# A new step table for a decoder trunk: heads at 0.7 of a step, and a router that takes four more steps

## The chip, the cores and the metric

The kernel runs on one core of a Trainium2 chip. Its time is the device time of one execution in microseconds (us), taken as the median of several runs. The core has five engines that run programs of their own and meet at semaphores: TensorE (PE), VectorE (DVE), ScalarE (ACT), GpSimd (POOL) and SyncE (SP), and 16 DMA engines that all queues share.

## The reference

The input x is 512 rows of 1024 columns, in float32. There are two layers. A layer takes x through a modulated RMS norm, a token mixer (six heads of dilated sliding-window attention, a diagonal state-space model on 256 channels, six heads of latent attention), an output projection and a gated residual, and then through an expert retrieval:

```python
def peer_ffn(h, wq, subkeys, u_tab, v_tab):
    q = (hf @ wq).reshape(T, PEER_HEADS, 2, PEER_DKEY // 2)
    scores = jnp.einsum('thjd,hjkd->thjk', q, subkeys)
    top_s, top_i = lax.top_k(scores, PEER_TOPK)                      # 8 heads, 2 sides, 16 of 128
    cand = top_s[:, :, 0, :, None] + top_s[:, :, 1, None, :]
    best_s, best_c = lax.top_k(cand.reshape(...), PEER_TOPK)         # 16 of the sums
    experts = i1 * PEER_KEYS + i2                                    # 128 experts for each row
    gates = softmax(best_s)
    act = gelu(einsum('td,tkd->tk', xt, u_tab[experts]))
    out = einsum('tk,tkd->td', gates * act, v_tab[experts])
```

Each row of x so reads 128 experts of 2048 numbers (a row of u and one of v, laid side by side in memory), in each of the two layers.

## The kernel before, in words

The 512 rows are 4 tiles of 128; with two layers there are 8 tiles of work, numbered 0 to 7 (`TILES`). A tile needs 128 gathers: gather n brings the n-th expert of each of its 128 rows, 128 x 2048 numbers, into one of the 8 places of a ring (`ringbuf`, `RING = 8`). POOL does nothing else (`pool_program`, L638): before gather n it waits until PE has finished with gather n - 8 (`summed`), and before the first gather of a lot until VectorE has written its indices (`idx_done`).

Two gathers are a pair, and a pair is a *step*: 64 steps a tile, 512 in all. For each pair VectorE takes the dot product of both u rows with the normed input (L1846) and a product with the gates (L1849), ScalarE makes of them the weight and two scaled diagonals (L1335 to L1350), and PE adds the two v rows into PSUM with these diagonals, 16 matmuls (L1003), which frees the two places of the ring. At the start of a tile's pairs the sums of the tile before are copied out (`sides`, L1853 and L1355), folded by PE (L1016) and finished by VectorE (L1861, L1862).

The rest of a tile's work (its norm, projections, state-space model, attention, output projection, query projection and scores, then the router, which picks the experts) lies between the pairs of the tile before: this is the *background*. Each of PE, ScalarE and VectorE has one generator `background()` that walks through `tile(j)` for all tiles in a fixed program order, and says by `yield at(j, step)` when its next piece is due. `at(j, step)` is `START[j] + step` in pair numbers. The engine's main loop issues a pair, and the `Feed` issues all background pieces whose due step has come, so a due step between two whole numbers counts as the next whole one; I call what stands between two pairs a slot. On PE the slot's background stands ahead of the slot's pair, on VectorE and ScalarE behind it. No piece overtakes another on its engine, also when the table gives it an earlier step. Everything due before step 0 is done before the first pair, one piece behind the other: the prologue.

`clocks()` gives for each tile its start and its *phase* (the step of its first own pair): phase j is 64 j, and with `LEAD = READY = 58` a tile starts 58 steps before its phase. In table steps of a tile: norm and transposes 0 to 3, projection by eight chunks of `w_in` 3 to 11 on PE and evacuated by ScalarE at 6 to 12, the state-space model on VectorE from 7 to 14, attention preparation to 18, then 12 attention heads in 14 iterations from 19 on, one per step: PE writes the logits of head i, transposes the weights of head i - 1 and mixes head i - 2 (L854, L862, L873), VectorE adds the bias and takes the maximum (L1669), ScalarE takes the exp (L1243) and evacuates the transposed weights (L1234). The bias comes by DMA, one block `BM` for each of the six window heads and one for the six latent ones, in two places, and SP loads block b when head b - 2 has been scored (`lmax`, L588). Behind the heads come the norm of the mix, the output projection, the second norm, and the query projection with its scores, one of eight chunks of `p_wq` each 1.5 steps. SP's queue is a fixed program too, driven by semaphores and not by the table: it loads a chunk as soon as PE has freed its place (`w_done`).

The router runs on VectorE (`route`). For each of 8 heads it takes the 16 best of 128 keys on both sides (two pieces) and the 16 best of the candidate sums (third piece, L1813 and `top16`); then for each lot of two heads (in tile 0 lots of 1, 1, 2, 2, 2) it works out indices and gates in three pieces (`batch`). `route_clock(j)` gives each piece its due step from a running sum of costs in table units: 1.7, 1.7 and 3.3 for a head, 1.0, 2.2 and 3.4 for a lot, 80.0 units for a tile and 86.6 for tile 0. Before, a piece is due at `44.5 + now / 3.14`, so all go at 3.14 units a step; a piece due more than a step behind the phase is put one step later. The router begins 13.5 steps ahead of the phase and is done 11.9 steps behind it (14.0 in tile 0). ScalarE's exp of a lot's gates (`gates`, L1098) is due with the lot's first piece; that of the last lot is merged into ScalarE's program of the next tile, behind head step 3. That next tile starts 6 steps behind the phase.

In tile 3's attention (`j == T - 1`, in the phase of tile 2) the tables of the second layer's state-space model are built: six pieces of `setup(1)` on VectorE from head 5 on, and three on ScalarE at heads 4, 6 and 10, the last with four passes over 128 x 1024 (L1078 to L1081).

## Time and profile before

| | |
|---|---|
| median of 3 runs | 3276.8 us (3274.89 to 3279.24) |
| the profiled execution, in all | 3276.72 us |
| its span, first to last instruction | 3274.9 us |
| busy in the span | PE 71%, VectorE 72%, ScalarE 44%, POOL 35% |
| moved by DMA | 1318.48 MB, 403 GB/s in the mean |
| mean granted clock of TensorE | 0.842 |

### The profile page before, as it was taken

Reading aid. Unit: us, or ns where it says so; the run is one execution under the profiler, and the core shown is the slowest. Engines: PE = TensorE matmul, PEld = TensorE weight load, DVE = VectorE, ACT = ScalarE, POOL = GpSimd, SP = SyncE. Lnnn points to the kernel's source line nnn. Section 1 sums busy time; section 2 is a strip of 40 time slices with the busy share of each in tenths; the row PEclk is TensorE's granted clock in tenths of the full one; section 3 lists DMA queues with packets and bytes.
Section 4 is the critical chain, followed back from the end, with each engine's and each line's share of the span. In section 5 each row is a group of like instructions: output and inputs, shape, how many; then the busy total and the mean of one; then the engine's idle time right before and its main releaser. Section 6 shows DMA issues by size and latency. Waiting matters only on the chain.

```text
span 3274.9 us, 44590 instructions
## 1 busy us (share of the span) xinstructions
PE 2328.0 (71%) x15012; PEld 1150.4 (35%) x15012; DVE 2369.8 (72%) x6467; ACT 1439.0 (44%) x4646; POOL 1143.5 (35%) x1029
## 2 busy tenths in 40 slices
PE   7675777677875777857676677768777577775555
PEld 5362334333442433514243233424335143431111
DVE  6669856797668876688667985688766986688554
ACT  2214454344533456344543445334553446434443
POOL 0003333333433333333443334333443333434443
PEclk9887889879987888869788788888889799877777
DMA  9859999999999999999999999999999999999998
GB/s 374 362 209 374 412 420 420 418 389 420 421 418 409 407 420 380 419 409 418 420 417 417 396 420 421 419 401 405 415 420 419 402 417 421 419 415 393 415 422 332
DMA packets 207467, 1318.48 MB, mean 403 GB/s; under 512 B 26413, under 2 KB 43613, under 8 KB 54150
## 3 DMA queue, kind: packets, MB, share of 16 engines
q0 software_dynamic: 147456, 1073.81, 79.7%
q1 hardware_dynamic: 58918, 241.04, 18.4%
q8 instruction: 119, 1.95, 0.2%
q10 hardware_dynamic: 864, 0.79, 0.1%
q14 instruction: 110, 0.90, 0.1%
HBM read 1310.54 MB, written 7.29 MB: 402 GB/s over the span
## 4 chain that ended last, share of the span: by engine, by line
DMA 38%; DVE 23%; PE 21%; ACT 6%; issue 4%; POOL 3%; ACTq 0%; SPq 0%; POOLq 0%; DVEq 0%
DMA ringbuf<-in_p_uv,IDX 34%; PE PS L1003 11%; DVE ringbuf L1846 11%; POOL ringbuf L638 3%; DMA WB<-in_p_wi 3%; PE PS L935 3%; PE PS L965 2%; PE PS L777 2%; ACT v_th L1338 2%; ACT DIAG L1350 1%; ACT v_w L1343 1%; DVE I L1739 1%; PE PS L736 1%; DVE T L1737 1%; DVE EQ L1783 1%
## 5 line engine op out<-in xcount | busy, mean ns | idle before, releaser
L638 POOL DMA_INDIRECT ringbuf<-in_p_uv,IDX x1024 | 1143.1, 1116 | 2105.9 <-PE PS L1003 1698.0
L1003 PE MATMUL PS<-ringbuf,DIAG 64*64 64x512 f32 x8192 | 1303.3, 764 | 776.0 <-ACT DIAG L1350 752.6
L1846 DVE SCALAR_TENSOR_TENSOR ringbuf<-ringbuf,H 128x1024 f32<-128x1024 f32 x1024 | 1237.5, 1222 | 618.2 <-DMA ringbuf<-in_p_uv,IDX 614.7
L1003 PEld LDWEIGHTS PS<-ringbuf,DIAG 64*64 64x64 f32 x8192 | 313.4, 158 | 1483.0 <-ACT DIAG L1350 1019.5
L1335 ACT ACTIVATE v_sq<-v_y 128x2 f32<-128x2 f32 x512 | 104.1, 203 | 1430.3 <-DVE ringbuf L1846 1430.2
L1343 ACT ACTIVATE v_w<-v_th,v_g 128x1 f32<-128x1 f32 x1024 | 340.5, 379 | 48.6 <-ACT v_th L1338 1.1
L1338 ACT ACTIVATE v_th<-v_sq,v_y 128x1 f32<-128x1 f32 x1024 | 340.5, 380 | 17.2
L1350 ACT ACTIVATE DIAG<-fold,v_w 128x64 f32<-128x64 f32 x1024 | 300.4, 340 | 16.6
L965 PEld LDWEIGHTS PS<-HT,WB 128*128 128x128 f32 x1856 | 227.4, 203 | 66.4 <-issue 61.4
L965 PE MATMUL PS<-HT,WB 128*128 128x128 f32 x1856 | 238.1, 290 | 0.1
L777 PE MATMUL PS<-WB,HT 128*128 128x256 f32 (+2 forms) x816 | 176.1, 371 | 48.7 <-DMA WB<-in_p_wi 43.8
L777 PEld LDWEIGHTS PS<-WB,HT 128*128 128x128 f32 x816 | 146.2, 197 | 102.8 <-DMA WB<-in_p_wi 67.3
L1669 DVE CUSTOM_DVE_ANT_0 PB<-PS,BM 128x128 f32<-128x128 f32 (+3 forms) x96 | 47.1, 491 | 84.0 <-PE PS L854 48.6
L1849 DVE TENSOR_TENSOR v_g<-v_y,GATE 128x2 f32<-128x2 f32 x512 | 82.5, 161 | 17.8
L1846 DVE DVE_READ_ACCUMULATOR ringbuf<-ringbuf,H 128x1 f32 x1024 | 84.0, 82 | 0.0
L1737 DVE MAX8 T<-SC 128x8 f32<-128x128 f32 x256 | 74.0, 289 | 4.4
L1243 ACT ACTIVATE PB<-PB,NMX 128x128 f32<-128x128 f32 (+3 forms) x96 | 53.0, 552 | 50.6 <-DVE NMX L1669 50.3
L1739 DVE FIND_INDEX8 I<-T,SC 128x8 uint32<-128x128 f32 x256 | 72.9, 285 | 0.0
L935 PE MATMUL PS<-KEEP,HT 128*128 128x256 f32 x256 | 60.7, 392 | 3.7 <-ACT HT L1273 3.7
L935 PE MATMUL PS<-WB,HT 128*128 128x256 f32 x256 | 59.2, 385 | 0.0
L935 PEld LDWEIGHTS PS<-KEEP,HT 128*128 128x128 f32 x256 | 48.6, 194 | 23.3 <-issue 17.0
L1234 ACT ACTIVATE PT<-PS 128x128 f32<-128x128 f32 (+3 forms) x96 | 40.3, 420 | 31.2 <-PE PS L862 31.0
(287 smaller groups left out, 2277.3 us busy)
## 6 DMA issues: line engine op xcount, KB each, us to landing
WB<-in_p_wq SPq DMA_DIRECT2D x58, 1024.0 KB, 12.3
WB<-in_p_wi SPq DMA_DIRECT2D x37, 1024.0 KB, 9.6
ringbuf<-in_p_ahead SPq DMA_DIRECT2D x24, 1024.0 KB, 12.2
WB<-in_p_wo SPq DMA_DIRECT2D x16, 1024.0 KB, 9.7
ringbuf<-in_p_uv,IDX POOLq DMA_INDIRECT x1024, 12.6
WB<-in_p_ada SPq DMA_DIRECT2D x12, 1024.0 KB, 12.7
WF<-in_p_ada SPq DMA_DIRECT2D x12, 1024.0 KB, 13.6
WB<-in_p_wi SPq DMA_DIRECT2D x14, 768.0 KB, 8.8
```

The costliest lines, as they stand in the source:

```text
L638: pool.indirect_dma_start(out=ring[n % RING], out_offset=None, in_=table, in_offset=bass.IndirectOffsetOnAxis(ap=IDX[:, k % 2, s:s + 1], a ...
L777: last = pe.matmul(PS[:, 4 + i % 2, 0:w], HT[:, k, :], weights(n)[:, k * w:(k + 1) * w], start=(k == 0), stop=(k == KD - 1))
L935: last = pe.matmul(PS[:, 6 + i % 2, 0:WIDE], HT[:, k, :], wt[:, k * WIDE:(k + 1) * WIDE], start=(k == 0), stop=(k == KD - 1))
L965: last = pe.matmul(PS[:, 4 + i % 2, h * P:(h + 1) * P], weights(n)[:, k * WIDE + h * P:k * WIDE + (h + 1) * P], HT[:, k, :], start=(k == 0 ...
L1003: mm = pe.matmul(PS[half:half + HALF, 2 * c + r, :], DIAG[r * HALF:(r + 1) * HALF, (n + q) % DIAGS, :], row[r * HALF:(r + 1) * HALF, D + c ...
L1335: act.activation(SQY[:, b, :], Y[:, b, :], ACT.Square, scale=GELU_S / GELU_T).then_inc(squared, 1)
L1338: th = link.mark(act.activation(TH[:, b, q:q + 1], SQY[:, b, q:q + 1], ACT.Tanh, scale=Y[:, b, q:q + 1], bias=Y[:, b, q:q + 1]))
L1343: w = link.mark(act.activation(W[:, b, q:q + 1], TH[:, b, q:q + 1], ACT.Identity, scale=G[:, b, q:q + 1], bias=G[:, b, q:q + 1]))
L1350: act.activation(DIAG[:, n % DIAGS, :], fold[:, :], ACT.Copy, scale=W[:, b, q:q + 1])\
L1737: step(dve.max(tops[:, part], values))
L1739: step(dve.max_index(places[:, part], tops[:, part], values))
L1846: dve.scalar_tensor_tensor(row, row, GELU_T, H2[:, k % 2, :], ALU.mult, ALU.mult, accum_out=Y[:, b, q:q + 1]).then_inc(dotted, 1)
```

## The change

Only the step table is changed; no instruction, load or semaphore is added or taken away.

- A tile starts 54 steps before its phase instead of 58 (`LEAD`, `READY`), so 10 steps behind the phase of the tile before.
- The iterations of the heads are due at `19 + 0.7 i` instead of `19 + i`. Counted from the phase they begin at -35 (before: -39) and end at -25.9 (before: -26).
- Everything behind the heads is due 4 table steps earlier, which is the same pair as before (on ScalarE and VectorE the norm of the mix, 32 and 33 before, is due at 28.2 and 29). What lies ahead of the heads keeps its table step, and so comes 4 pairs later.
- The router begins at the same pair, 13.5 steps before the phase. Its first 42 units go at 3.5 units a step, the rest at 2.15. It ends 15.6 steps behind the phase (18.7 in tile 0), before 11.9 (14.0).

```diff
--- before.py
+++ after.py
@@ -170,10 +170,11 @@
     return start, phase
 
 
-LEAD = 58
-READY = 58
+LEAD = 54
+READY = 54
 PERIOD = 64
-ROUTE_RATE = 3.14
+HEAD_STEP = 0.7
+ROUTE_FROM, ROUTE_FAST, ROUTE_SLOW, ROUTE_EARLY = 40.5, 3.5, 2.15, 42.0
 START, PHASE = clocks()
 
 
@@ -188,7 +189,8 @@
 
     def piece(cost):
         nonlocal now
-        at_, now = at(j, 44.5 + now / ROUTE_RATE), now + cost
+        steps = min(now, ROUTE_EARLY) / ROUTE_FAST + max(now - ROUTE_EARLY, 0.0) / ROUTE_SLOW
+        at_, now = at(j, ROUTE_FROM + steps), now + cost
         return at_ + 1 if at_ > PHASE[j] + 1 else at_
 
     for h in range(PH):
                     last.then_inc(omm, 1)
 
                 for i in range(2 * HEADS + 2):
-                    yield at(j, 19 + i)
+                    yield at(j, 19 + HEAD_STEP * i)
                     if i == 0:
                         pe.wait_ge(mla_ev, 3 * (j + 1))
                     if j == 0 and i in (5, 9):
@@ -903,7 +905,7 @@
                         mix(i - 2)
                     if i in (3, 4):
                         side_rows(i - 3)
-                yield at(j, 34)
+                yield at(j, 30)
                 if j == 0:
                     reduce_ahead(3)
                 for c in more[-2:]:
@@ -917,7 +919,7 @@
                     if k % 4 == 3:
                         last.then_inc(mx_tp, 1)
                 for i in range(4):
-                    yield at(j, 35 + i)
+                    yield at(j, 31 + i)
                     if i < KEPT:
                         pe.wait_ge(keep_in, 16 * KEPT * (l + 1))
                         wt, used = KEEP[:, i, :], keep_done
@@ -935,7 +937,7 @@
                         last = pe.matmul(PS[:, 6 + i % 2, 0:WIDE], HT[:, k, :], wt[:, k * WIDE:(k + 1) * WIDE],
                                          start=(k == 0), stop=(k == KD - 1))
                     last.then_inc(used, 1)
-                yield at(j, 41)
+                yield at(j, 37)
                 if j == 0:
                     reduce_ahead(4)
                 pe.wait_ge(n2_h, j + 1)
@@ -956,7 +958,7 @@
                     last.then_inc(s_mm, 1)
 
                 for i in range(PH):
-                    yield at(j, 42 + 1.5 * i)
+                    yield at(j, 38 + 1.5 * i)
                     m, n = PH * j + i, number[("wq", j, i)]
                     pe.wait_ge(w_in[slot[n]], turn[n])
                     pe.wait_ge(q_ev, m - 1) if i >= 2 else pe.wait_ge(n2_ev, 2 * (j + 1))
@@ -970,7 +972,7 @@
                         score(i - 1)
                     if j == 0 and i == 5:
                         reduce_ahead(5)
-                yield at(j, 42 + 1.5 * PH)
+                yield at(j, 38 + 1.5 * PH)
                 score(PH - 1)
 
             def background():
@@ -1235,7 +1237,7 @@
 
                 tables = setup(1) if j == T - 1 else None
                 for i in range(2 * HEADS + 2):
-                    yield at(j, 19 + i)
+                    yield at(j, 19 + HEAD_STEP * i)
                     if tables and i in (4, 6, 10):
                         next(tables, None)
                     if i < 2 * HEADS:
@@ -1254,15 +1256,15 @@
                         ada_keep(more[i - 2], 4 + (i - 1) % 2)
                     if 1 <= i <= len(more):
                         ada_take(more[i - 1])
-                yield at(j, 32)
+                yield at(j, 28.2)
                 for c, lo, hi in ((0, 0, SWA), (1, SWA, SWA + S5C), (2, SWA + S5C, D)):
                     act.wait_ge(at_fin, 2 * j + (1, 1, 2)[c])
                     act.activation(SQ[:, lo:hi], HM[:, lo:hi], ACT.Square, accum_out=V0[:, c:c + 1]).then_inc(mx_ss, 1)
-                yield at(j, 33)
+                yield at(j, 29)
                 act.wait_ge(mx_rs, j + 1)
                 for c, lo, hi in ((0, 0, SWA), (1, SWA, SWA + S5C), (2, SWA + S5C, D)):
                     act.activation(HM[:, lo:hi], HM[:, lo:hi], ACT.Copy, scale=RS[:, c:c + 1]).then_inc(mx_n, 1)
-                yield at(j, 34)
+                yield at(j, 30)
                 if j == 0:
                     keep_ahead(3)
                 if tables:
@@ -1272,10 +1274,10 @@
                         act.wait_ge(mx_tp, 2 * j + k // 4 + 1)
                     act.activation(HT[:, k, :], PS[:, 4 + k // 4, k % 4 * P:(k % 4 + 1) * P], ACT.Copy,
                                    scale=LP[:, LP_MIX + k:LP_MIX + k + 1]).then_inc(mx_ev, 1)
-                yield at(j, 39)
+                yield at(j, 35)
                 act.wait_ge(wo_res, 4 * (j + 1))
                 act.activation(SQ[:, :], XM[:, j % 2, :], ACT.Square, accum_out=VN[:, 1:2]).then_inc(n2_ss, 1)
-                yield at(j, 41)
+                yield at(j, 37)
                 if j == 0:
                     keep_ahead(4)
                 for b in range(2):
@@ -1290,7 +1292,7 @@
 
                 due = [(lot[0], g) for g, lot in enumerate(route_clock(j)[1][:-1])]
                 for i in range(PH + 1):
-                    step = at(j, min(42.5 + 1.5 * i, 42 + 1.5 * PH))
+                    step = at(j, min(38.5 + 1.5 * i, 38 + 1.5 * PH))
                     while due and due[0][0] <= step:
                         b, g = due.pop(0)
                         yield b
@@ -1647,7 +1649,7 @@
 
                 tables = setup(1) if j == T - 1 else None
                 for i in range(2 * HEADS):
-                    yield at(j, 19 + i)
+                    yield at(j, 19 + HEAD_STEP * i)
                     if i == 0:
                         dve.wait_ge(s5_th, j + 1)
                         dve.scalar_tensor_tensor(G5[:, :, :], SQ5[:, :, :], 1.0, YT[:, :, :], ALU.add, ALU.mult)\
@@ -1673,9 +1675,9 @@
                     add_ahead(j, KD // 2)
                     if 2 <= i <= len(more) + 1 and more[i - 2][2] // 4 == 4:
                         row_gain(more[i - 2], 4 + (i - 1) % 2)
-                yield at(j, 32)
+                yield at(j, 28.2)
                 finish(1)
-                yield at(j, 33)
+                yield at(j, 29)
                 dve.wait_ge(mx_ss, 3 * (j + 1))
                 link(dve.tensor_tensor(V0[:, 0:3], V0[:, 0:3], CPK[:, CP_MEANS + 33:CP_MEANS + 36], ALU.mult))
                 link(dve.tensor_scalar(V0[:, 0:3], V0[:, 0:3], EPS, None, ALU.add))
@@ -1684,7 +1686,7 @@
                 if j == 1:
                     column_scale(1)
                 for i in range(4):
-                    yield at(j, 36 + i)
+                    yield at(j, 32 + i)
                     cols = slice(i * WIDE, (i + 1) * WIDE)
                     if i < KEPT:
                         dve.wait_ge(keep_done, KEPT * j + i + 1)
@@ -1697,7 +1699,7 @@
                     link(dve.tensor_tensor(res, PS[:, 6 + i % 2, 0:WIDE], MOD[:, 0, cols], ALU.mult))
                     dve.tensor_tensor(XM[:, j % 2, cols], XM[:, j % 2, cols], res, ALU.add).then_inc(wo_res, 1)
                     add_ahead(j, (3, 3, 2, 0)[i])
-                yield at(j, 40)
+                yield at(j, 36)
                 h2 = H2[:, j % 2, :]
                 dve.wait_ge(n2_ss, j + 1)
                 link(dve.tensor_scalar(VN[:, 1:2], VN[:, 1:2], 1.0 / D, EPS, ALU.mult, ALU.add))
```

## Rows read from the trace of the kernel before

**Rows 1.** The page, section 2: GB/s moved in 40 equal slices.
```profile
GB/s 374 362 209 374 412 420 420 418 389 420 421 418 409 407 420 380 419 409 418 420 417 417 396 420 421 419 401 405 415 420 419 402 417 421 419 415 393 415 422 332
```

**Rows 2.** The page: gather queue (section 3); gather issues, us to landing (section 6).
```profile
q0 software_dynamic: 147456, 1073.81, 79.7%
...
ringbuf<-in_p_uv,IDX POOLq DMA_INDIRECT x1024, 12.6
```

**Rows 3.** Stretches: length, PE, PEld, DVE, ACT, POOL busy, clock, DMA, GB/s.
```profile
257.00:344.00 87.00, 57.54 (x341) 27.14 (x342) 77.17 (x250) 37.92 (x123) 31.73 (x28) 0.79 0.94 377
645.00:726.00 81.00, 56.85 (x324) 22.73 (x317) 76.09 (x240) 36.45 (x115) 30.53 (x28) 0.75 0.97 387
1027.00:1105.00 78.00, 53.94 (x324) 22.00 (x315) 74.24 (x234) 35.99 (x114) 29.85 (x28) 0.78 0.98 396
1415.00:1501.00 86.00, 57.17 (x321) 23.01 (x314) 76.28 (x239) 36.52 (x115) 26.14 (x26) 0.70 1.01 408
1802.00:1883.00 81.00, 55.59 (x336) 23.61 (x332) 75.54 (x236) 36.42 (x115) 29.56 (x28) 0.79 1.00 397
2182.00:2261.00 79.00, 55.75 (x320) 22.45 (x313) 74.80 (x235) 36.41 (x115) 30.17 (x28) 0.76 0.98 389
2562.00:2641.00 79.00, 55.54 (x328) 22.60 (x321) 74.74 (x236) 36.34 (x115) 28.54 (x28) 0.78 0.99 399
2938.00:3010.00 72.00, 43.38 (x229) 9.60 (x220) 68.69 (x216) 28.70 (x94) 26.79 (x26) 0.69 0.99 397
```

**Rows 4.** Stretches: heads, then query weights in tile 1's phase; tables in tile 2's.
```profile
792.00:855.00 63.00, 50.42 (x320) 22.62 (x312) 38.60 (x88) 37.47 (x119) 26.28 (x24) 0.89 1.02 420
944.00:1027.00 83.00, 56.49 (x394) 31.39 (x396) 62.03 (x200) 30.11 (x101) 26.64 (x24) 0.84 1.01 419
1244.00:1266.00 22.00, 13.39 (x86) 6.98 (x82) 12.82 (x35) 17.70 (x46) 8.50 (x8) 0.84 0.72 279
```

**Rows 5.** Timeline of VectorE in tile 1's phase: start us, us, instruction.
```profile
649.60 0.28 DVE L1737 MAX8 T<-SC 128x8 f32<-128x128 f32 x1
...
653.02 1.21 DVE L1846 SCALAR_TENSOR_TENSOR ringbuf<-ringbuf,H 128x1024 f32<-128x1024 f32 x1
...
655.49 0.34 DVE L1813 TENSOR_TENSOR CA<-T 128x64 f32<-128x64 f32 x2
...
657.50 1.21 DVE L1846 SCALAR_TENSOR_TENSOR ringbuf<-ringbuf,H 128x1024 f32<-128x1024 f32 x1
...
710.27 0.18 DVE L1752 TENSOR_TENSOR GATE<-B 128x32 f32<-128x32 f32 x1
...
711.95 1.22 DVE L1846 SCALAR_TENSOR_TENSOR ringbuf<-ringbuf,H 128x1024 f32<-128x1024 f32 x1
...
714.43 0.68 DVE L1780 TENSOR_TENSOR EQ<-B2f,CPK 128x512 f32<-128x512 f32 x1
...
719.60 1.22 DVE L1846 SCALAR_TENSOR_TENSOR ringbuf<-ringbuf,H 128x1024 f32<-128x1024 f32 x1
```

**Rows 6.** Timeline in tile 2's phase: POOL's next gather; ScalarE around its tables.
```profile
1256.97 0.94 POOL L638 DMA_INDIRECT ringbuf<-in_p_uv,IDX  x1 [9.96 <-PE PS L1003]
...
1242.26 1.28 ACT L1078 ACT_TABLE_LOAD   x1
...
1249.05 0.72 ACT L1243 ACTIVATE PB<-PB,NMX 128x512 f32<-128x512 f32 x1
```

**Rows 7.** Tile BM: us from issue to landing.
```profile
DMA to landing us min/median/max: 3.7/7.7/16.4
```

**Rows 8.** Timeline of PE in two wide tiles: head and pair instructions.
```profile
1232.98 2.07 PE L854 MATMUL PS<-KTM,QTM 96*128 96x512 f32 x2
...
1236.45 1.95 PE L1003 MATMUL PS<-ringbuf,DIAG 64*64 64x512 f32 x16
...
2757.78 1.12 PE L854 MATMUL PS<-KTM,QTM 96*128 96x512 f32 x2
...
2759.18 1.00 PE L873 MATMUL PS<-VM,PT 128*128 128x64 f32 x8
```

## Prediction

> **What bounds the kernel now.** I read the slices of the page first, then the queues, then stretches of single tiles, then single instructions. The GB/s row stands near 420 in almost every slice [rows 1]: the kernel is bound by the bytes it moves. The gather queue alone has 1073.81 MB for 1024 gathers, 1.05 MB each [rows 2]; at 420 GB/s that is 2.50 us a gather and 4.99 us for a step (a pair of gathers). So the time can fall only where the rate dips. It dips once per tile, from a tile's phase on: each row of [rows 3] is the stretch from a phase to about 14 or 15 steps behind it, and its length times (1 - GB/s / 420) is what the queues lost there. For tiles 0 to 7 in turn that is 8.9, 6.4, 4.5, 2.5, 4.4, 5.8, 4.0 and 3.9 us, together 40.4 us. VectorE is busy 89 to 95% in those rows, between instructions that wait for each other, so it has no idle time: it sets the pace there. Later stretches of tile 1 run at 420 and 419 GB/s with VectorE at 61 and 75% [rows 4]. The one other dip is the table setup in tile 2's phase: 279 GB/s, 22 x (1 - 279/420) = 7.4 us [rows 4]. The slow ends of the span (209 GB/s in the prologue, 332 at the end) are not touched.
>
> Why VectorE sets the pace: a pair takes it 2.47 us from start to the next work (653.02 to 655.49), a router head 3.42 us for its two sides (649.60 to 653.02) and 2.01 us for the candidates (655.49 to 657.50), and a lot of two heads 1.68 us (710.27 to 711.95) and 5.17 us (714.43 to 719.60) [rows 5]. A tile's router is then 8 x 5.43 + 4 x 6.85 = 70.8 us for its 80 table units, 0.885 us a unit. At the old rate of 3.14 units a step a step costs 2.47 + 2.78 = 5.25 us, over the 4.99 that the gathers need.
>
> **The change, part by part.** No instruction and no byte is added or removed; the price is all in where things meet.
>
> *Router, front.* From 13.5 steps before a phase the rate is 3.5 units a step, up to 42 units (12 steps): 2.47 + 3.10 = 5.57 us a step. The query weights stream there, and a step lasts 83 / 12 = 6.9 us [rows 4]. Cover 1.3 us a step; cost nothing. Without the cover it would be 0.6 us x 12 = 7 us a tile. The scores that it waits for are issued at unmoved steps, the first half a step ahead of it and later ones further ahead, so no wait appears.
>
> *Router, tail.* By the phase 45.2 units are done, against 42.4; the other 34.8 go at 2.15 a step: 2.47 + 1.90 = 4.37 us, now under 4.99. Over 12 steps VectorE gains about 0.6 us a step on the queues and no longer loses 0.26. The first steps also carry the copy of the sums and the finish of the tile before, which don't move; the queues must still drain and refill across that boundary. Tiles 1 to 7 lost 31.5 us; I take 70% back, 22 us. Bounds: nothing (the dip is that of the boundary and of the next tile's projection chain) and all 31.5.
>
> *The next tile's first steps* (norm, projection, state-space part) start 4 steps later, as does the end of the router (15.6 instead of 11.9 steps into the phase, for 80 units): their overlap is the same, and SP's projection chunks move with the PE steps that free them. Cost nothing; if the ring is fuller when they begin, a little better. Tile 0 is different: its router has 86.6 units, and its last gates on ScalarE are due 17.2 steps in, with the evacuations of steps 16, 17 and 18 queued behind them in program order; before they were due 13.0 steps in with one evacuation behind. PE's third projection chunk (step 17) waits for the first of those evacuations, and PE's pair 17 stands behind it. On VectorE the first rotation, due 17, stands behind the router's end at 18.7. So of tile 0's 8.9 us I take 3 back; bounds: -4 (two steps of stalls, less than ring and chunks in flight cover) and +8.9.
>
> *Heads at 0.7.* They begin 4 steps later and end where they did. Steps are rounded up to pairs, so slots 22, 24 and 26 hold two heads. VectorE and ScalarE have room. PE: a pair 1.95 us, and a wide head at full clock from 2757.78 to the end of its last matmuls, 2.4 us [rows 8]: 1.95 + 2.4 / 0.7 = 5.4 us a step over 8.4 steps, 3 us behind the queues in the widest tiles (3 and 7), less in the others. In a double slot PE also waits for ScalarE's exp of that very slot, some 1.5 us more, each time with the slot's pair behind it. The bias rows BM are the tighter wait: a load goes out when the head two earlier has been scored and lands 7.7 us later (median) [rows 7]. Two heads were 10 us apart, now 7: heads 3 to 6 make VectorE wait 1 to 3 us each, about 6 in all, with the pair's dots queued behind and ScalarE and PE behind those. What hides it is the ring: a gather lands 12.6 us after its issue against 2.5 us of transfer [rows 2], so some 9 us of late consumption leave the queues fed. The lag adds up to 6 to 9 us at worst. I charge 3 us over all tiles; bounds 0 and 7.4 us a tile (below).
>
> *Tables in tile 2's phase.* VectorE's six setup pieces fall in 4 slots instead of 6, so the lag grows by about 2 steps' slack, (4.99 - 2.47) x 2 = 5 us; against that ScalarE's block of 6.8 us (1242.26 to 1249.05) [rows 6], now in the slot of VectorE's two last pieces, runs beside them instead of behind them. I charge 2 us, bounds -7.4 (dip gone) and +7.
>
> Sum: 3274.9 - 22 - 3 + 3 + 2 = 3254.9 us of span; that execution took 3276.7 in all, 1.8 us around its span, and so does the median, 3276.8. So 3257 us.
>
> A rule that speaks against this: the array drops to its half clock when waits for data break up its work (the Trainium skill, "TensorE: Matmul & The Clock Gate", section "HAM oscillation — how this bites in real kernels"). By it the new waits in double slots would slow the very heads that are now denser. The trace agrees only in part: the head stretch stands at a clock of 0.89 in spite of its gaps.
>
> **Rivals.**
> *A, forecast (0.60).* Gain 12 to 34 us.
> *B, the chain moves along (0.20).* The dip comes from the boundary and from the next tile's transposes, first projection and ScalarE's evacuation, which are only shifted. For: PE and ScalarE wait for each other at just those steps. Against: VectorE has no idle time there. A quarter of 31.5 comes back, 8, less 3 + 2 and plus 1 in tile 0: 3273.
> *C, the head stretch outruns the ring (0.11).* Place: slots 22 to 26 in tiles 1 to 7. It decides once pairs are consumed more than about 10 us late, at the BM wait of the fourth head plus the double slots. Price from the one place where it happens: the gather queue had no release for 9.96 us [rows 6] and the queues lost 7.4 us. Seven times 7.4 = 52 on top of the forecast without its charge of 3: 3257 - 3 + 52 = 3306, slower. For: the queues show no reserve once that gap opens. Against: there ScalarE stood still for 6.8 us at once behind a VectorE that was already late; here the delays are 1 to 3 us each, with slots of one head between them.
> *D, the clock (0.02).* A head's logits take 2.07 us at the half clock, 1.12 at full [rows 8], 1.85 times. At 1.85 x (1.95 + 3.43) = 9.9 us a step the widest two tiles fall 41 us behind each, less 9 of ring: 3257 + 64 = 3321.
> *E, nothing (0.07).* Gain in the phase and loss in the heads cancel, 3 us in each of seven tiles: 3257 - 3 + 21 = 3275.
>
> **How the numbers follow.** About 0.2%, 6.6 us, is what can be told from no change. Faster: A's 0.60 and three quarters of B's 0.20, 0.75. Same: the rest of B's and most of E's, 0.11. Slower: C, D and a little of E, 0.14. The likeliest case alone gives 3242 to 3265; with B and E the range goes to 3242 to 3277; C and D lie outside with 0.13, the far end of A with a few hundredths.
>
> **What would show it.** Right: the stretches of 14 steps behind each phase at 410 GB/s or more, VectorE waiting for gathers there, and the head stretches still at 418 to 420. Tile 0's stretch shows a longer wait of PE for ScalarE's projection evacuations. VectorE's waits for BM become more and longer without a dip. The forecast is wrong if the phase stretches stay at 385 to 400 GB/s (B), or if the five steps from slot 22 of each tile drop under 400 (C), or if the clock there falls under 0.75 (D).

## The result, and the profile after

The changed kernel takes 3329.4 us (median of 4 runs, 3324.29 to 3332.72) against 3276.1 for the kernel before on the same chip: a ratio of 1.0161, 95% interval 1.0148 to 1.0173. It is 53 us slower; repeated later on another chip (below), it was 50 us slower, so differences between kernels here carry some 3 to 5 us. Its profiled execution took 3329.18 us, its span 3327.4; before 3274.9. Forecast were 3257 us and faster, so the direction was wrong.

Lines of the changed kernel stand two higher than those of before (L1003 is now L1005). The GB/s row of its page, which answers to [rows 1]:

```profile
GB/s 373 365 194 384 388 398 396 406 416 420 406 413 406 412 418 303 416 398 408 414 399 419 400 412 419 399 407 410 420 396 419 409 410 416 391 412 409 419 421 330
```

Many slices that stood at 417 to 421 now stand at 396 to 412, and the sixteenth (tile 2's phase, heads of tile 3) at 303. Where, by stretches, with the columns of [rows 3]: first eight that begin at a phase and go to the same step as there, then those that answer to [rows 4].

```profile
257.00:334.00 77.00, 40.64 (x228) 11.87 (x229) 68.67 (x219) 34.16 (x109) 27.27 (x25) 0.69 0.93 381
661.00:735.00 74.00, 43.04 (x245) 11.35 (x242) 64.23 (x198) 34.72 (x110) 31.32 (x28) 0.76 0.99 406
1043.00:1116.00 73.00, 43.52 (x240) 11.37 (x240) 63.50 (x195) 33.92 (x108) 30.91 (x28) 0.71 0.99 405
1450.00:1533.00 83.00, 44.94 (x244) 11.65 (x240) 64.16 (x196) 34.27 (x108) 27.70 (x28) 0.71 0.98 397
1843.00:1919.00 76.00, 44.44 (x243) 11.78 (x244) 64.54 (x197) 34.80 (x110) 31.36 (x28) 0.75 0.99 399
2227.00:2300.00 73.00, 42.21 (x240) 11.30 (x240) 63.20 (x195) 33.75 (x107) 31.29 (x28) 0.78 0.99 405
2611.00:2683.00 72.00, 38.33 (x236) 10.58 (x240) 62.86 (x192) 33.20 (x105) 29.89 (x28) 0.83 0.99 407
2993.00:3059.00 66.00, 36.46 (x224) 8.88 (x224) 58.28 (x169) 29.13 (x95) 31.67 (x28) 0.81 0.97 400
801.00:870.00 69.00, 53.00 (x342) 23.58 (x334) 47.63 (x122) 37.40 (x118) 26.45 (x23) 0.84 1.02 420
962.00:1043.00 81.00, 54.45 (x368) 29.66 (x360) 62.76 (x207) 29.29 (x98) 24.86 (x22) 0.78 1.01 419
1269.00:1297.00 28.00, 22.99 (x146) 11.83 (x146) 19.85 (x63) 21.60 (x53) 10.85 (x11) 0.88 0.78 298
```

Most phase stretches did get better (406, 405 and 407 for tiles 1, 5 and 6, where [rows 3] have 387, 389 and 399), though none reached the 410 that the forecast asked for, and tile 3's fell from 408 to 397. The tables' stretch of the same steps grew from 22 to 28 us.

A table by steps tells where the rest went. For each step between two of VectorE's pairs I took its length less its bytes at 420.5 GB/s, the flat part of the row, from the records of all DMA packets, and summed over the tiles. This is DMA time lost, in us, in one profiled execution of each kernel; "head" is what lies ahead of tile 0's phase.

```
steps behind phase  0-4   4-14  14-20  20-29  29-40  40-48  48-64  head   all
before             18.9   22.4    2.2    3.3    7.9    1.0   21.8  61.6  139.3
changed            25.8    3.6   14.8    3.6   29.0   29.1   20.7  65.0  191.7
difference         +6.9  -18.8  +12.6   +0.3  +21.1  +28.1   -1.1  +3.4  +52.4
```

The sum is that of the spans, 52.5 us, and has to be, since the bytes are the same; what the table tells is the place. In the repeat of the changed kernel the sections are within 2 us of these, but for 18.0 at 14 to 20, so a difference of 3 us in one section can be chance. (Ahead of the phase of tile 0 the loss lay between 59.1 and 66.8 us in all kernels here, 64.8 in one that changes nothing there, so I don't read the 3.4.) At 4 to 14 18.8 us came back, but 19.5 us are lost again on either side. What is left over is the stretch of the heads (29 to 40) and the norm of the mix with the output projection (40 to 48), which the forecast had at 3 us, and 2 for the tables. At 40 to 48 it is 3.4 to 4.9 us in each of tiles 0 to 6. In tile 1, first the kernel before, then the changed one:

```profile
876.00:921.00 45.00, 35.22 (x208) 18.75 (x208) 28.51 (x65) 20.57 (x66) 16.96 (x16) 0.89 1.01 420
```

```profile
892.00:937.00 45.00, 33.73 (x192) 18.30 (x192) 27.79 (x63) 21.35 (x69) 17.22 (x15) 0.87 0.98 387
```

The timeline of the changed kernel shows what happens at its start (start us, us, instruction, and in brackets the idle time before it and what ended it):

```profile
887.76 1.95 PE L1005 MATMUL PS<-ringbuf,DIAG 64*64 64x512 f32 x16
887.93 0.56 DVE L1645 TENSOR_TENSOR HM<-PS,RDN 128x384 f32<-128x384 f32 x1 [2.46 <-PE PS L875]
...
888.52 0.52 ACT L1262 ACTIVATE SQ<-HM 128x384 f32<-128x384 f32 x1
...
889.17 0.16 DVE L1682 TENSOR_TENSOR V<-V,CPK 128x3 f32<-128x3 f32 x1 [0.68 <-ACT SQ L1262]
...
891.72 1.22 DVE L1848 SCALAR_TENSOR_TENSOR ringbuf<-ringbuf,H 128x1024 f32<-128x1024 f32 x1
891.83 1.52 ACT L1266 ACTIVATE HM<-HM,RS 128x384 f32<-128x384 f32 x3 [2.69 <-DVE RS L1383]
...
893.41 1.09 PE L918 MATMUL PS<-CPK,HM 128*128 128x128 f32 x8 [3.71 <-ACT HM L1266]
...
896.45 3.69 PE L1005 MATMUL PS<-ringbuf,DIAG 64*64 64x512 f32 x16 [1.95 <-ACT DIAG L1352]
...
900.41 1.32 POOL L640 DMA_INDIRECT ringbuf<-in_p_uv,IDX  x1 [8.26 <-PE PS L1005]
```

Before, the squares were due at step 32 and the root and the scaling at 33, with a pair between them. Now 28.2 and 29 both round up to 29. So in one slot VectorE waits for the last head's mix and finishes it (L1645), ScalarE squares it, VectorE takes the root and only then the pair's dots (L1848), ScalarE scales and only then turns to the pair, and PE transposes ahead of its pair. Two pairs of PE are 8.7 us apart (887.76 and 896.45), and POOL gets no release for 8.26 us. ScalarE's scaling waited 5.9 us in all for the root in the kernel before and 21.3 us here (8 waits each).

PE's clock has a part in this. The last two pairs ahead of the output projection and its first chunk, in the same stretch of the kernel before, and the last such pair of the changed one (columns of [rows 3]):

```profile
876.01 2.85 PE L1003 MATMUL PS<-ringbuf,DIAG 64*64 64x512 f32 x16 [3.02 <-ACT DIAG L1350]
...
881.06 1.95 PE L1003 MATMUL PS<-ringbuf,DIAG 64*64 64x512 f32 x16 [0.45 <-ACT DIAG L1350]
883.33 3.69 PE L935 MATMUL PS<-KEEP,HT 128*128 128x256 f32 x16 [0.32 <-ACT HT L1273]
```

```profile
896.45:900.14 3.69, 3.69 (x17) 0.87 (x17) 1.95 (x6) 3.53 (x14) 0.00 (x0) 0.50 1.01 424
```

In the changed kernel PE had stood idle for 3.71 and 1.95 us with 1.09 us of transposes between, and the pair ran at a granted clock of 0.50. Before, the slow pair was the last but one in five of the tiles 1 to 7 and the last in two; now it is the last in all seven (3.35 to 3.69 us), and the projection's first chunk behind it takes up to 4.71 us, before 3.69 to 3.72. The last three pairs, the transposes and that chunk took PE 88.8 us in these tiles before and 96.0 here, so in this stretch the clock can account for some 7 us of the changed kernel's loss. In the kernel below with the norm's slot alone changed it is 105.6 us, 17 more than before.

### The profile page after: what moved, and what is told of

Its sections match the earlier page's. It is cut to its first block, busy times and chain, and to the rows that moved or that the text cites. A ratio compares the mean times of both kernels' runs of the same rounds, so it can differ in the third digit from the quotient of the medians.

```text
span 3327.4 us, 44589 instructions
## 1 busy us (share of the span) xinstructions
PE 2326.9 (70%) x15012; PEld 1154.3 (35%) x15012; DVE 2362.1 (71%) x6467; ACT 1439.5 (43%) x4646; POOL 1151.7 (35%) x1029
## 3 DMA queue, kind: packets, MB, share of 16 engines
q8 instruction: 119, 1.95, 0.2%
## 4 chain that ended last, share of the span: by engine, by line
DMA 37%; PE 25%; DVE 19%; ACT 7%; issue 4%; POOL 3%; SPq 1%; ACTq 0%; DVEq 0%; POOLq 0%
DMA ringbuf<-in_p_uv,IDX 31%; PE PS L1005 13%; DVE ringbuf L1848 9%; PE PS L937 3%; PE PS L779 3%; POOL ringbuf L640 3%; PE PS L967 2%; ACT v_th L1340 2%; DMA BM<-skew 2%; DMA WB<-in_p_wi 2%; ACT DIAG L1352 2%; ACT v_w L1345 1%; DMA WB<-in_p_ada 1%; DMA WB<-in_p_wq 1%; PE PS L738 1%
## 5 line engine op out<-in xcount | busy, mean ns | idle before, releaser
L1005 PE MATMUL PS<-ringbuf,DIAG 64*64 64x512 f32 x8192 | 1289.6, 757 | 754.5 <-ACT DIAG L1352 734.4
L1848 DVE SCALAR_TENSOR_TENSOR ringbuf<-ringbuf,H 128x1024 f32<-128x1024 f32 x1024 | 1234.9, 1221 | 541.2 <-DMA ringbuf<-in_p_uv,IDX 536.6
L1005 PEld LDWEIGHTS PS<-ringbuf,DIAG 64*64 64x64 f32 x8192 | 311.5, 158 | 1478.7 <-ACT DIAG L1352 1017.4
L1340 ACT ACTIVATE v_th<-v_sq,v_y 128x1 f32<-128x1 f32 x1024 | 340.5, 380 | 17.2
L1848 DVE DVE_READ_ACCUMULATOR ringbuf<-ringbuf,H 128x1 f32 x1024 | 84.4, 82 | 0.0
L864 PE MATMUL PS<-CPK,PB 128*128 128x128 f32 x240 | 48.8, 305 | 41.9 <-ACT PT L1236 41.8
L1699 DVE TENSOR_TENSOR HM<-PS,MOD 128x256 f32<-128x256 f32 x32 | 13.6, 424 | 75.5 <-PE PS L937 75.5
L937 PEld LDWEIGHTS PS<-KEEP,HT 128*128 128x128 f32 x256 | 51.4, 207 | 25.8 <-issue 18.6
## 6 DMA issues: line engine op xcount, KB each, us to landing
WB<-in_p_wq SPq DMA_DIRECT2D x58, 1024.0 KB, 12.7
WB<-in_p_wo SPq DMA_DIRECT2D x16, 1024.0 KB, 12.6
```

Of the source, the lines that this page charges most:

```text
L937: last = pe.matmul(PS[:, 6 + i % 2, 0:WIDE], HT[:, k, :], wt[:, k * WIDE:(k + 1) * WIDE], start=(k == 0), stop=(k == KD - 1))
L1005: mm = pe.matmul(PS[half:half + HALF, 2 * c + r, :], DIAG[r * HALF:(r + 1) * HALF, (n + q) % DIAGS, :], row[r * HALF:(r + 1) * HALF, D + c ...
L1340: th = link.mark(act.activation(TH[:, b, q:q + 1], SQY[:, b, q:q + 1], ACT.Tanh, scale=Y[:, b, q:q + 1], bias=Y[:, b, q:q + 1]))
L1848: dve.scalar_tensor_tensor(row, row, GELU_T, H2[:, k % 2, :], ALU.mult, ALU.mult, accum_out=Y[:, b, q:q + 1]).then_inc(dotted, 1)
```

## The experiments

Ratios are to the kernel before, run on the same chip; "us less than the changed kernel" compares ratios with the first measurement, 1.0161, and would be 5 us smaller against the repeat's 1.0146. Losses are those of the table above, in us, first for the sections that matter, then over all steps.

**Which part costs.**

The kernel before with the heads of the changed one:

```diff
-                    yield at(j, 19 + i)
+                    yield at(j, 23 + 0.7 * i)
-                yield at(j, 32)     # squares, finish(1)
+                yield at(j, 32.2)
```

> The table of before with only the heads changed: they start at 23 instead of 19 and follow at 0.7 of a step, and the norm of the mix is due at 32.2 and 33, so all of it falls in the same pairs as in the changed kernel. Start of a tile and router as before. In the traces the stretch from 29 to 48 steps behind a phase loses 58 us of DMA time in the changed kernel against 9 in the one before. Theory 1 (the heads, the norm and the projection behind them make the whole loss): 3276 + 45 to 55, so 3321 to 3331 us. Theory 2 (the later start of a tile and the slow router tail push everything and the heads only show it): within 8 us of 3276.

Measured: 1.0109 (1.0092 to 1.0126), 35 us over before. Losses at 29 to 40 and 40 to 48: 29.1 and 28.4, the same as in the changed kernel. So the heads' part carries about two thirds of the slowdown by itself, with the router and the tile's start untouched; the time lies between the two theories. Not all of the loss in the heads reaches the end: at 0 to 20 this kernel lost 37.6 us, 6 less than the one before.

The changed kernel with the router at its old rate:

```diff
-ROUTE_FROM, ROUTE_FAST, ROUTE_SLOW, ROUTE_EARLY = 40.5, 3.5, 2.15, 42.0
+ROUTE_FROM, ROUTE_FAST, ROUTE_SLOW, ROUTE_EARLY = 40.5, 3.14, 3.14, 42.0
```

> The changed kernel with its router at the old single rate of 3.14 units a step. Theory 1 (the new rates give back what VectorE lost behind each phase, 18.8 us from step 4 to 14, and the heads are to blame for the rest): 3329 + 10 to 19, so 3339 to 3348 us. Rival (what the rates give back from step 4 to 14 is lost again from 0 to 4 and from 14 to 20, 43.5 us in sum before and 44.2 after): within 6 us of 3329. If the slow tail itself does harm, below 3323.

Measured: 1.0127 (1.0110 to 1.0144). Losses at 0 to 4, 4 to 14 and 14 to 20: 14.1, 9.7 and 19.0, together 42.8, against 44.2 with the new rates and 43.5 before. The new rates move the loss and take nothing off it; in time they cost 6 to 11 us (1.0127 against 1.0146 and 1.0161). And this kernel shows what the late start does by itself: with the router's rate unchanged, 12.7 us at 4 to 14 come back, two thirds of the changed kernel's 18.8, and 16.8 us more are lost at 14 to 20 (the dense heads without the late start, the kernel above, leave 20.5 and 2.4 there).

The changed kernel with the norm in two slots again, the squares due a slot ahead of the root:

```diff
-HEAD_STEP = 0.7
+HEAD_STEP = 0.69
-                yield at(j, 28.2)
+                yield at(j, 28)
```

> The changed kernel with the heads at 0.69 and the norm of the mix due at 28 and 29, so that the last head, the finish and the squares fall in slot 28, and the root and the scaling in slot 29, where the changed kernel has all of them in slot 29. Theory 1a (the norm's chain through three engines in one slot starves the gather queue and the projection behind it, with PE above the queues' pace, cannot win it back: 28 us from step 40 to 48): 3300 to 3312 us. Rival 1b (PE's lag out of the double slots does it, wherever the norm stands): 3322 to 3332 us.

Measured: 1.0103 (1.0086 to 1.0120), 19 us less than the changed kernel, as the first theory said; the loss at 40 to 48 falls from 29.1 to 11.0.

The changed kernel with tile 3's steps up to the norm, and tile 2's router, by the old table:

```diff
+def sooner(j, step):     # at every step up to 18
+    return at(j, step) - (4 if j == 3 else 0)
-                    yield at(j, 19 + HEAD_STEP * i)
+                    yield sooner(j, 19 + i) if j == 3 else at(j, 19 + HEAD_STEP * i)
+        steps = now / 3.14 if j == 2 else steps
```

> The changed kernel, but tile 3 by the old table: it starts 58 steps ahead of its phase, its heads are a step apart, and the router of tile 2 goes at the old rate. Tile 3 is the one with the table setup among its heads. Theory 1 (head stretch): the phase of tile 2 loses 24.4 us from step 29 to 48 in the changed kernel and 7.7 before, so 17 us come back: 3309 to 3315 us. Rival (the dip there is that of the setup alone and the density is no matter): within 5 us of 3329.

Measured: 1.0085 (1.0068 to 1.0102), 25 us less, where the theory had 17. Tile 2's loss at 29 to 40 goes from 19.5 to 9.3 (before 7.7), the section's sum from 29.0 to 14.9. In tile 3 the last head now stands in slot 28, and the finish, the squares, the root and the scaling still share slot 29: yet the loss of tile 2's phase at 40 to 48 goes from 4.9 to 0.0, and the pair behind runs in 1.95 us. This one case suggests that the last head's matmuls in the same slot are what makes the chain too long.

What tile 2's phase looks like in the changed kernel: VectorE and POOL in tile 3's heads, then ScalarE's tables.

```profile
1232.12 0.69 DVE L1671 CUSTOM_DVE_ANT_0 PB<-PS,BM 128x512 f32<-128x512 f32 x1 [7.08 <-DMA BM<-skew]
...
1240.22 0.69 DVE L1671 CUSTOM_DVE_ANT_0 PB<-PS,BM 128x512 f32<-128x512 f32 x1 [4.92 <-DMA BM<-skew]
...
1249.19 0.94 POOL L640 DMA_INDIRECT ringbuf<-in_p_uv,IDX  x1 [17.92 <-PE PS L1005]
...
1276.76 1.28 ACT L1080 ACT_TABLE_LOAD   x1
...
1283.79 0.94 POOL L640 DMA_INDIRECT ringbuf<-in_p_uv,IDX  x1 [10.51 <-PE PS L1005]
```

Two heads in a row wait 7.08 and 4.92 us for their bias, with the pairs queued behind, and the gathers stand still for 17.92 us; the table block that [rows 6] show then costs its 10.5 us as before. Over the whole kernel the waits for BM grew only from 32.1 us (9 of them) to 36.2 (11): they bite where two fall together in the widest tile.

**The norm alone, half of the change, one clump.**

The changed kernel once more, on another chip:

> The changed kernel itself, beside the next three on their chip. All theories: 1.6% over the kernel before, as the first time.

Measured: 1.0146 (1.0129 to 1.0163).

The kernel before with one edit: the last iteration of the heads, the finish and the squares share the slot of the root and the scaling.

```diff
-                    yield at(j, 19 + i)
+                    yield at(j, 19 + i if i <= 2 * HEADS else 32.2)
-                yield at(j, 32)
+                yield at(j, 32.2)
```

> The kernel before with one thing changed: the last iteration of the heads and the finish of the mix are due half a step later, so that they share a slot with the root and the scaling of the norm (slot 33), as in the changed kernel. Heads a step apart, router and start as before. Theory 1a (this chain of three engines in one slot, ahead of four projection steps in which PE needs 5.5 us a step, makes the loss from step 40 to 48): 15 to 28 us over the kernel before. Rival 1b (it hurts only where dense heads have already used up the ring): within 5 us of the kernel before.

Measured: 1.0069 (1.0052 to 1.0086), 22.4 us. Every head up to the last stands where it was, and the loss at 40 to 48 is 28.6, in the changed kernel 29.1; that at 29 to 40 is 7.3, before 7.9. Tile 1's stretch, and ScalarE's waits for VectorE's root:

```profile
883.00:927.00 44.00, 34.57 (x192) 19.14 (x192) 27.94 (x64) 20.45 (x66) 17.64 (x15) 0.84 0.98 390
...
  ACT HM L1264: 21.2, 8
```

Half the late start, with the router at 3.14 and the norm in two slots:

```diff
-LEAD = 54
-READY = 54
-HEAD_STEP = 0.7
+LEAD = 56
+READY = 56
+HEAD_STEP = 0.845      # and all behind the heads 2 table steps later
```

> Half of the change: a tile starts 56 steps ahead of its phase, the heads follow at 0.845 (one slot with two heads instead of three), the norm of the mix stands in its two slots as before, the router goes at the old rate. Theory 1 (loss grows with the slots that hold two heads and with the norm in one slot; none of it is due to the later start as such): within 8 us of the kernel before. Theory 2 (each step that a tile starts later costs): half of the loss with the old router rate, 20 us over the kernel before.

Measured: 1.0014 (1.0003 to 1.0026). A late start by two steps, with heads that are denser to match, costs 5 us; the losses grew most in tile 2 (12.6 at 29 to 40, before 7.7). The two are not separated here.

The changed kernel with a lot's third piece one slot later where all three shared one:

```diff
-            lots.append([piece(cost) for cost in (1.0, 2.2, 3.4)])
+            lot = [piece(cost) for cost in (1.0, 2.2, 3.4)]
+            if math.ceil(lot[2]) == math.ceil(lot[0]):
+                lot[2] += 1
+            lots.append(lot)
```

> The changed kernel, but where all three pieces of a router lot are due in one slot, the third goes one step later. It is so for the second lot of tiles 1 to 7, in the slot 3 ahead of the phase: VectorE is 6.9 us in it, that slot lasts 11.5 us, and POOL gets no place for 8 us. Theory 1 (this clump is why the first four steps of a phase lose 25.8 us in the changed kernel and 14.1 with the old rate): 7 to 12 us less than the changed kernel, 3317 to 3322 on the first chip's scale. Rival (the loss there is the boundary's own, the drain of the sums): within 4 us of the changed kernel.

Measured: 1.0156 (1.0135 to 1.0178): nothing. The loss at 0 to 4 is 25.0. The theory that this one clump costs the steps at the phase falls.

**Do the costs add, and the front.**

The kernel before with dense heads and the norm left in slots 32 and 33:

```diff
-                    yield at(j, 19 + i)
+                    yield at(j, 23 + 0.69 * i)
```

> The kernel before with the heads due at 23 + 0.69 i and everything behind them at its old step, so that ScalarE's and VectorE's norm of the mix stays in two slots (32 and 33). The dense heads alone, without the norm pressed into one slot. Theory 1 (two costs that add): 8 us less than the dense heads with the norm in one slot is not enough, the norm in one slot was 22 us, so this one stands 10 to 16 us over the kernel before, with the loss of steps 40 to 48 back at 1 to 3 us (it was 28.4) and the loss of steps 29 to 40 at 20 us or more, most of it in tile 2. Rival (one cost, the norm; the dense heads are free without it): within 5 us of the kernel before, steps 29 to 40 at 8 to 12. Rival (ring left emptier by the dense heads, whatever the norm does): 25 us or more over it, steps 40 to 48 still above 10.

Measured: 1.0071 (1.0055 to 1.0087), 26 us; I had expected 10 to 16, and the last rival holds. Losses at 29 to 40 and 40 to 48: 31.0 (tile 2: 14.3) and 15.3. So the dense heads cost by themselves as much as the norm did, and the two overlap: 26 and 22 us apart, 35 together. With the norm in two slots the projection stretch still loses 1.3 to 4.2 us in six phases of the seven (none in tile 3's), which fits a ring that the heads hand over already late; how full the ring was is not measured.

The changed kernel with a short fast front:

```diff
-ROUTE_FROM, ROUTE_FAST, ROUTE_SLOW, ROUTE_EARLY = 40.5, 3.5, 2.15, 42.0
+ROUTE_FROM, ROUTE_FAST, ROUTE_SLOW, ROUTE_EARLY = 40.5, 3.5, 2.45, 28.0
```

> The changed kernel, with the router's fast rate of 3.5 only for the first 28 units (8 steps, which end when the query weights have streamed) and 2.45 from there, so it is done at nearly the same step as in the changed kernel. Theory 1 (the fast rate past the last query weights puts VectorE behind before the phase, and the first four steps pay): 5 to 10 us under the changed kernel's 1.0161, so a ratio of 1.013 to 1.0145 over the kernel before, with the loss of steps 0 to 4 at 18 to 21 us instead of 25. Rival (the four late steps at the phase are due to the boundary work alone): the loss of steps 0 to 4 stays at 24 to 26 and the ratio within 0.001 of 1.016. Rival (more of the router falls behind the phase, 39 units instead of 35, and that costs): steps 4 to 20 lose 4 to 8 us more, and the time is level or above.

Measured: 1.0085 (1.0069 to 1.0100), 25 us less than the changed kernel where I had expected 5 to 10. Losses at 0 to 4, 4 to 14 and 14 to 20: 3.8, 4.0 and 9.8, together 17.6 instead of 44.2. Four steps behind tile 5's phase, first in the changed kernel, then here:

```profile
2227.00:2247.00 20.00, 13.50 (x72) 3.25 (x72) 18.42 (x50) 9.43 (x31) 8.87 (x9) 0.77 0.92 366
```

```profile
2206.00:2225.00 19.00, 11.29 (x68) 2.66 (x60) 18.35 (x50) 7.43 (x23) 7.30 (x8) 0.82 1.01 421
```

In tiles 1 to 7, of which the forecast spoke, the loss at 0 to 20 is 11.7 us, 34.1 before: its 22 us are there, with the late start and a tail nearly as sparse, and with the long front they are not (32.2). They are not there in every kernel with this router, though: see the kernel with half the late start, and the last one, below.

All mends found so far (norm apart, tile 3 by the old table, the lot spread), with the long front:

> The changed kernel with three mends at once: the norm of the mix apart from the last head (step 0.69, norm at 28 and 29), tile 3's part up to the heads and tile 2's router by the old table, and a lot's third piece one slot later where it fell into the slot of the first. Theory (the costs add): 1.0161 less 0.0058 (norm apart) less 0.0076 (tile 3) less 0: ratio 1.002 to 1.005, 3283 to 3294 us. Rival (both mends work on the same late ring, so they overlap): 1.006 to 1.009. Rival (what is left is the router alone, which should gain what the prediction said once the heads do no harm): below 1.000.

Measured: 1.0048 (1.0033 to 1.0064), as expected: the costs add, nearly.

The kernel before with only a gentler router (3.5 for 28 units, then 2.8) and ScalarE's long table block moved behind the last head:

```diff
+        steps = min(now, 28) / 3.5 + max(now - 28, 0) / 2.8 if j else now / 3.14
-                    if tables and i in (4, 6, 10):
+                    if tables and i in (4, 6):
...
+                    if tables and i == 2 * HEADS:     # behind evac(i - 1)
+                        next(tables, None)
```

> The kernel before with its heads and its start untouched and two edits. The router goes at 3.5 units a step for its first 28 units and at 2.8 behind them (3.14 all along before; tile 0 unchanged), and ScalarE's longest table block in tile 3's attention moves from head step 10 to behind the last evacuation of the heads. Theory: the router's part takes 3 to 8 us back in steps 0 to 14 of tiles 1 to 7 (rate down from 5.25 to 4.95 us a step), the tables 4 to 7 us in tile 2's steps 29 to 40 (7.7 us lost there before); together ratio 0.995 to 0.998. Rival (what is taken from one slot is met again in the next: the phase's dip belongs to the boundary): ratio 0.999 to 1.001, with the tables alone to be seen in tile 2. Rival (the block now delays the norm of the mix behind it, and the projection starts late in tile 3): steps 40 to 48 of tile 2 lose 5 us or more, ratio 1.000 or above.

Measured: 0.9995 (0.9985 to 1.0004): nothing. Losses at 0 to 20 are 44.0, before 43.5. In tile 2 the block's 7.7 us at 29 to 40 turned into 4.9 there and 3.6 at 40 to 48: it met the norm of the mix, as the last rival said.

**What in the front costs, and can the change pay.**

The changed kernel with the fifth head's three pieces one slot later:

```diff
-        heads.append([piece(cost) for cost in (1.7, 1.7, 3.3)])
+        heads.append([piece(cost) + (1 if h == 4 and j else 0) for cost in (1.7, 1.7, 3.3)])
```

> The changed kernel with one edit: in tiles 1 to 7 the three pieces of the router's fifth head are due one slot later (slots -1, 0 and 1 of the phase instead of -2, -1 and 0). No other rate or step moves. By the slots of its table VectorE then has 11.7 us of router work in slots -4 to 0 where the changed kernel has 14.6 and the kernel with the short front 10.2. Theory (the loss of steps 0 to 4 is VectorE's lag at the moment when the query weights stop, set by what lies in the slots just before the phase): the loss of steps 0 to 4 falls from 25 to 10 to 17 us, the time by 8 to 14 us, ratio 1.012 to 1.0135 over the kernel before. Rival (what the short front gained came from the tail's rate of 2.45, not from the front): the loss of steps 0 to 4 stays at 23 to 26, ratio 1.0155 to 1.017. Rival (the work is met again one slot on): 0 to 4 falls, 4 to 14 rises by as much, ratio as before.

Measured: 1.0155 (1.0139 to 1.0170), loss at 0 to 4 25.1. The theory fell. The first rival, that the gain came from the tail's rate, would give just this; the next kernel rules it out.

The changed kernel with the tail at 2.45 and the long front kept, so that nothing moves up to slot 1:

```diff
-ROUTE_FROM, ROUTE_FAST, ROUTE_SLOW, ROUTE_EARLY = 40.5, 3.5, 2.15, 42.0
+ROUTE_FROM, ROUTE_FAST, ROUTE_SLOW, ROUTE_EARLY = 40.5, 3.5, 2.45, 42.0
```

> The changed kernel with the tail's rate alone changed, 2.45 units a step instead of 2.15; the fast front of 42 units stays. Up to slot 1 behind the phase every piece of the router lies in the same slot as in the changed kernel. Theory (the slots just before the phase, with 14.7 us of router work in slots -5 to -1, cause the loss of steps 0 to 4; it takes both clumps away, not one, to mend it): the loss of steps 0 to 4 stays at 23 to 27 us and that of 14 to 20 falls from 15 to 8 to 12 since the router ends 1.6 steps sooner; ratio 1.0135 to 1.0155. Rival (the short front's gain came from the tail's rate): the loss of steps 0 to 4 falls under 10 and the ratio to 1.008 to 1.010. Rival (a tail of 4.64 us a step is too fast on top of a long front): 1.0165 or more.

Measured: 1.0245 (1.0229 to 1.0262), 27 us more than the changed kernel. Only the last rival had the direction, and its floor of 1.0165 is far below. But the kernel separates front and tail: the loss at 0 to 4 stays (30.7, with the short front and the same tail 3.8), so it is the front's; the loss at 14 to 20 goes from 14.8 to 41.1, and where it arises can be read. Tile 5 of this kernel:

```profile
2315.07 0.94 POOL L640 DMA_INDIRECT ringbuf<-in_p_uv,IDX  x1 [0.30 <-issue]
...
2321.13 1.15 ACT L1118 ACTIVATE HM<-XM,RN 128x1024 f32<-128x1024 f32 x1 [10.04 <-DVE RN L1383]
...
2322.33 1.97 PE L729 MATMUL PS<-CPK,HM 128*128 128x128 f32 x8 [9.24 <-ACT HM L1118]
2324.50 2.91 PE L1005 MATMUL PS<-ringbuf,DIAG 64*64 64x512 f32 x16 [0.20 <-ACT DIAG L1352]
...
2328.46 1.01 POOL L640 DMA_INDIRECT ringbuf<-in_p_uv,IDX  x1 [12.46 <-PE PS L1005]
```

and the same place in the changed kernel:

```profile
2293.84 1.15 ACT L1118 ACTIVATE HM<-XM,RN 128x1024 f32<-128x1024 f32 x1 [5.04 <-DVE RN L1383]
...
2295.04 1.97 PE L729 MATMUL PS<-CPK,HM 128*128 128x128 f32 x8 [4.24 <-ACT HM L1118]
...
2301.94 1.15 POOL L640 DMA_INDIRECT ringbuf<-in_p_uv,IDX  x1 [8.48 <-PE PS L1005]
```

The next tile's first norm needs a root from VectorE, which stands behind whatever router pieces are due before it. ScalarE waits for the root with its pair behind, and PE waits for ScalarE with its own pair behind. Summed over tiles, ScalarE waited there 35.5 us in the kernel before, 37.2 in the changed one, 29.6 with the short front and 73.1 here.

Half the late start with the short front:

```diff
-ROUTE_FROM, ROUTE_FAST, ROUTE_SLOW, ROUTE_EARLY = 42.5, 3.14, 3.14, 42.0
+ROUTE_FROM, ROUTE_FAST, ROUTE_SLOW, ROUTE_EARLY = 42.5, 3.5, 2.45, 28.0     # tile 0: 3.14
```

> The version with half the late start (a tile starts 56 steps before its phase, heads 0.845 of a step apart, norm of the mix in two slots), which alone measured 1.0014, with the router of the short front: 3.5 units a step for 28 units, 2.45 behind them; tile 0's router at 3.14. Theory (the two are independent: the router gains 20 to 26 us in steps 0 to 20, the heads cost what they cost there): 1.0014 less 0.0064, ratio 0.994 to 0.9965, 3258 to 3265 us, losses of steps 0 to 20 at 16 to 22 us. Rival (the next tile begins two steps sooner here than with the short front and meets the router's last six steps, so the dip returns at steps 8 to 14): ratio 0.998 to 1.000, steps 4 to 14 at 12 us or more.

Measured: 0.9999 (0.9990 to 1.0008): 5 us better than with the router at 3.14, not 21. Losses at 0 to 20: 30.3, and 10.0 of them at 0 to 4, where the full late start with the same short front had 3.8.

The same with tile 3 up to its heads and tile 2's router by the old table (the `sooner` above, with 2 for 4):

> The same version with tile 3 kept at the old table up to its heads (start 58 before the phase, heads a step apart) and tile 2's router at 3.14, since tile 2's phase holds the tables of the second layer. Theory: tile 2's steps 29 to 40 lose 7 to 8 us again instead of 12 to 13, its steps 0 to 20 lose 4 instead of 1 to 2: 2 to 4 us better than without this edit, ratio 0.993 to 0.996. Rival (tile 2's dip is the setup's own and does not follow the table): 2 to 3 us worse than without it.

Measured: 0.9986 (0.9977 to 0.9995), 3271.95 us against 3277.25 (27 runs). This is the one version whose interval lies below the kernel before, by 5 us, less than the 0.2% that I called measurable. It is the best of 17 kernels, so part of it may be chance.

The kernel before with the router alone changed:

```diff
+        steps = min(now, 28) / 3.5 + max(now - 28, 0) / 2.6 if j else now / 3.14
```

> The kernel before with its start, heads and norm untouched, and only the router changed: 3.5 units a step for 28 units, then 2.6 (the version with 2.8 had no gain; 3.14 before); tile 0 as before. VectorE: 2.47 + 2.6 x 0.885 = 4.77 us a step behind the front, under the 4.99 of the queues by 0.2. By its slots VectorE has 11.7 us of router work in slots -4 to 0 (before 14.7, with 2.8 14.6). Theory (what counts is the work in those slots and a rate below the queues' by more than a tenth or two): steps 0 to 4 lose 8 to 12 us instead of 19, steps 4 to 14 15 to 20 instead of 22, ratio 0.995 to 0.997. Rival (the gain of the short front needs the late start of the next tile, since the router's end now meets the next tile's projections from step -6 + 14 on): steps 4 to 20 lose more than before and the ratio is 0.999 to 1.002.

Measured: 1.0013 (1.0004 to 1.0022). Losses at 0 to 20 are 40.4, at 20 to 29 11.4 (before 3.3). The rival that the gain needs the late start holds in its result; the loss at 0 to 4, 17.2, did not go away either, though this kernel has the short front.

The changed kernel's start with the short front (3.5 for 28 units, then 2.45), the norm in two slots and tile 3 by the old table:

> The changed kernel's start (54 steps before the phase) with every mend found: the router 3.5 units a step for 28 units and 2.45 behind them, the norm of the mix apart from the last head, and tile 3's part up to the heads with tile 2's router by the old table. Theory (the costs add): the version with the mends and the long front measured 1.0048; the short front took 0.0076 off the changed kernel in seven tiles, six of them here: less 0.0065, ratio 0.997 to 0.9995, 3267 to 3276 us; steps 0 to 4 lose 4 to 8 us, steps 29 to 48 25 or so. Rival (half the late start is the better half): 0.9995 to 1.002. Rival (the heads' cost comes from the ring left empty at the boundary and goes with it): below 0.995.

Measured: 1.0019 (1.0008 to 1.0029). Losses at 0 to 20 28.9, at 29 to 48 26.4, in a profiled execution 6 us faster than the median. The rival that half the late start is the better half has the right time. The router's gain shrank: in tiles 1 to 7 23.2 us are lost at 0 to 20, where the same router beside the unmended heads had 11.7. Tile 2's router at the old rate explains 3 of these. Part of the gain at the phase thus belongs to kernels that lose time in the heads; why stays open.

## Why the prediction was wrong, point by point

- *The bound.* Right: outside the places named here both kernels stand near 420 GB/s. That VectorE alone set the pace at 4 to 14 is not borne out. With the old rates and the late start it is as busy there as before (94% before and 95% in tile 1's phase), and yet that stretch lost 9.7 us instead of 22.4.
- *The step that failed: "Heads at 0.7 ... I charge 3 us over all tiles", and with it the norm of the mix.* Where the sum has +3 and +2 for heads and tables, the table has +49.2 us at 29 to 48; where it has -22 and -3 for the router, +0.7 at 0 to 20. The charge listed double slots for the heads and overlooked that the norm's steps 28.2 and 29 round to the same slot as well: the note on them was in the change's description and got no cost. That alone is 22 us (the norm in one slot on the kernel before), of which the wait and PE's clock behind it were not separated; the dense heads without it are 26 us, both together 35 us. The cover was misjudged too: "some 9 us of late consumption leave the queues fed" was worked out for one delay with a full ring. Here up to three delays follow each other (bias, double slots, norm) ahead of steps that take PE 5.5 us at the full clock (a pair 1.95 us and a chunk of the output projection 3.69 us, which overlap a little) against the 4.99 of the queues, so PE cannot win back what is lost there: 15.3 us are lost at 40 to 48 with dense heads even when the norm has its two slots, 1.0 before.
- *Router, front: "cost nothing".* Failed, and this is why the router's 22 us did not show: in tiles 1 to 7 the loss at 0 to 20 went from 34.1 to 32.2 us only. The last byte of the query weights is read 17.2 us ahead of tile 5's phase, in slot -3 (before: 16.7), and the fast rate went on to 1.5 steps before the phase. The loss at 0 to 4 is 25.8 and 30.7 us with the long front and two tails, 3.8 with the short one. How it comes about stays open. By the table's slots, at the forecast's 0.885 us a unit, VectorE has 8.8 us of router in slots -3 to -1 in the changed kernel, 8.8 with the lot spread, 7.3 with the fifth head later, and 5.8 with the short front, which lost least. But the short front on the kernel before also has 5.8 there and loses 17.2, and the kernel before has 8.7, with an empty slot -5 ahead of it, and loses 18.9. So the work in these slots alone does not decide it.
- *Router, tail: 22 us.* Reached in one kernel only, the short front on the changed kernel: 22.4 us in tiles 1 to 7. The mechanism, a rate of VectorE below that of the queues, does not suffice: tails of 4.95 and 4.77 us a step with the old start gained nothing (0.9995 and 1.0013). Rival B (the chain moves along) holds in large part: the late start alone took 12.7 us off steps 4 to 14 and put 16.8 on 14 to 20, where the root of the next tile's norm is waited for.
- *Tile 0: 3 us back.* Named the right wait. PE's third projection chunk waited for ScalarE's first evacuation and POOL with it:

```profile
363.44 6.41 PE L779 MATMUL PS<-WB,HT 128*128 128x256 f32 x16 [11.96 <-ACT PRJ L1166]
...
372.32 0.95 POOL L640 DMA_INDIRECT ringbuf<-in_p_uv,IDX  x1 [18.40 <-PE PS L1005]
```

  Tile 0's losses went from 9.6 to 12.1 us at 0 to 20: 2.5 us worse instead of 3 better, within the bounds given (-4 to +8.9), with the dense heads' 8.8 at 29 to 48 on top.
- *Tables: 2 us.* 12 us (19.5 against 7.7 in tile 2 at 29 to 40), over the upper bound of 7. The tables' own block did not grow (10.51 us without a release, 9.96 before); the bias waits ahead of it did, up to 17.92 us without a gather. With dense heads on the kernel before it is 13.7, so the late start adds to it.
- *Rival C, at 0.11, was the one that came nearest.* Its place (double slots and the bias wait) is real in tile 2; in the other tiles the ring was outrun some slots later, at the norm, at 3.4 to 4.9 us a tile instead of 7.4. Its own sign, under 400 GB/s in the five steps from slot 22, shows in tiles 1 and 3 (399 and 308) and not in the other five (405 to 420). Its 3306 was 23 us short, about the router's gain that it kept; that the rest fits is luck, since the price was taken from another wait at another place.
- *Rival D* does not hold for the heads of tile 1, which stand at a granted clock of 0.84, before 0.89 [rows 4], with 420 GB/s; the five steps from slot 22 fell to 0.72 in tile 3 only (0.83 before). At the norm of the mix, which the rival did not name, half-clock pairs moved next to the projection, for some 7 us more of PE's time over tiles 1 to 7; how much of that reached the kernel's time no run separates. The rule of the Trainium skill weighed in the forecast ("TensorE: Matmul & The Clock Gate", section "HAM oscillation — how this bites in real kernels") would make the new waits slow PE down; at the norm this trace agrees (3.69 us for 1.95), though PE waits there for ScalarE and not for data of a DMA. The span's mean went from 0.842 to 0.830 only.

## What to carry to other kernels

When fractional due times are rounded to slots, write out each slot's contents on all engines, before and after, and look for a chain of waits (produce, reduce, scale, transpose) that used to have a slot boundary in it; pieces of an in-order engine that share a slot put their whole latency in front of what is queued behind. Slack in a ring is spent once: charge consecutive delays against it as a sum, and put the ones that used to be hidden next to each other in one line. A gain made at the bound (the tail) is kept only if the same work does not cost more where it is moved to. Here the sparser tail alone gained nothing, the late start alone moved the loss, and only with a short front did the two give back 22 us in one kernel: such edits have to be measured singly and together.

## What the runs showed of the hardware that was not expected

- A pair's 16 matmuls (L1005) do not have one price. They took 1.95 us at 887.76 and 3.69 us at 896.45 above, behind idle time. In the kernel before all 111 pairs of over 3.5 us ran at a granted clock of 0.5, and all 300 under 2.05 us at 1.0; 209 of 512 pairs took longer than 2.3 us, in the changed one 195. The count hides the place: from 4 slots before a phase to 12 behind it, 76 of 119 pairs are such in either kernel, and the mean there is 2.88 and 2.89 us, so the clock explains no difference there; right ahead of the output projection it went from 2 of 7 to 7 of 7.
- A wait of POOL for a place of the ring has no price of its own. In slots -8 to -2 of tile 5's phase POOL of the kernel before waited 5.66, 4.92, 5.52, 4.67 and 5.52 us, and all slots from -8 to -1 lost 0.9 us together (419 GB/s from 2130 to 2165 us, with query weights in the queues for all but the last of the waits). Waits of 5.63 and 4.04 us at steps 9 and 10 went with a loss of 3.1 us at steps 9 to 11 (352 GB/s from 2231 to 2244 us).
